# The first expert pair's gather written channel-major in two halves, with the router's sums ahead of the kept rows, the expert totals in a bank of their own and one early weight chunk moved up

## The reference

```python
h = h + cross_attn(rmsnorm(h, norm_xattn), ...)
h = h + moe(rmsnorm(h, norm_moe), lw)
# moe: logits = x @ w_router + b_router; top 4 of 32; softmax over the 4
# each expert e, on its own tokens:
gu = xb @ w_gate_up[e] + b_gate_up[e]        # 1024 -> 2048
gate, up = split(gu); glu = min(gate, 7) * sigmoid(1.702 * min(gate, 7))
y = ((clip(up, -7, 7) + 1) * glu) @ w_down[e] + b_down[e]   # 1024 -> 1024
out[token] += gate_weight * y
```

## Time and profile before

| | us |
|---|---|
| timed runs | 1409.6, 1412.96, 1413.68 |
| their median | 1412.96 |
| the profiled execution's span, first to last instruction | 1407.9 |
| from the first expert stage to the end, in that execution | 485.7 to 1407.9 |
| PE busy (matmul), share of the span | 98% |
| DMA, mean rate over the span | 353 GB/s |

### The profile page before, as it was taken

How to read it: one execution, slowest core, us unless ns; L and a number is a source line. 1 busy time by engine, 2 the same in 40 slices (tenths; PEclk the granted TensorE clock), 3 DMA queues, 4 the chain that set the end, 5 groups by cost and what they waited for, 6 DMA issues and landing times.

```text
span 1407.9 us, 16140 instructions
## 1 busy us (share of the span) xinstructions
PE 1376.7 (98%) x6438; PEld 673.5 (48%) x6438; DVE 441.5 (31%) x902; ACT 217.9 (15%) x403; POOL 27.9 (2%) x48
## 2 busy tenths in 40 slices
PE   9999999999999999999999999999999999999997
PEld 7788887677757633333333333333333332332322
DVE  5634345871461312221211312212113121121213
ACT  2220022052123411110101111011011010110102
POOL 0000002200000000000000000000000000000000
PEclk9999999999999999999999999999999999999999
DMA  7644446975379799999999999999999999999995
GB/s 256 210 154 154 175 142 200 376 268 190 118 283 398 284 413 428 429 425 430 427 430 427 430 427 429 428 429 429 428 428 429 430 427 430 427 430 426 431 426 228
DMA packets 71575, 497.25 MB, mean 353 GB/s; under 512 B 8752, under 2 KB 10216, under 8 KB 46824
## 3 DMA queue, kind: packets, MB, share of 16 engines
q1 hardware_dynamic: 65180, 477.94, 82.5%
q0 software_dynamic: 4432, 15.53, 3.0%
q10 hardware_dynamic: 1924, 3.23, 0.7%
HBM read 488.61 MB, written 8.24 MB: 353 GB/s over the span
## 4 chain that ended last, share of the span: by engine, by line
PE 83%; DMA 14%; DVE 2%; issue 1%; ACT 0%; SPq 0%; DVEq 0%
PE bank L1492 78%; DMA ring<-in_w_gate_up 8%; DMA flat<-in_w_gate_up 6%; PE bank L1503 4%; DVE wide L1418 1%; DMA flat<-in_x_prompt 0%; DVE wide L1475 0%; ACT wide L618 0%; PE bank L1946 0%; ACT L628 0%; ACT L658 0%; ACT wide L609 0%; SPq L506 0%; DVE wide L1466 0%; DVE wide L1395 0%
## 5 line engine op out<-in xcount | busy, mean ns | idle before, releaser
L1492 PE MATMUL bank<-ring,wide 128*64 128x512 f32 (+2 forms) x1696 | 405.5, 595 | 6.9 <-DMA ring<-in_w_gate_up 6.0
L1492 PE MATMUL bank<-wide 128*64 128x512 f32 (+6 forms) x1024 | 283.3, 574 | 8.7 <-DVE wide L1418 6.3
L1492 PE MATMUL bank<-tokT,ring 128*128 128x264 f32 x1152 | 266.0, 389 | 0.8 <-DVE tokT L959 0.8
L1492 PEld LDWEIGHTS bank<-ring,wide 128*64 128x64 f32 (+2 forms) x1696 | 132.4, 140 | 259.9 <-issue 246.1
L1492 PEld LDWEIGHTS bank<-tokT,ring 128*128 128x128 f32 x1152 | 217.8, 191 | 42.4 <-issue 6.4
L1492 PEld LDWEIGHTS bank<-wide 128*64 128x64 f32 (+4 forms) x1024 | 94.6, 152 | 171.9 <-issue 121.9
L609 ACT ACTIVATE wide<-bank 64x512 f32<-64x512 f32 (+3 forms) x104 | 58.2, 560 | 348.3 <-PE bank L1492 227.0
L1442 DVE TENSOR_SCALAR wide<-bank 128x512 f32<-128x512 f32 x32 | 22.1, 692 | 274.3 <-PE bank L1492 274.3
L1492 PE MATMUL bank<-flat,wide 128*64 128x512 f32 (+2 forms) x408 | 92.3, 589 | 3.7 <-DMA flat<-in_w_gate_up 3.7
L1492 PE MATMUL bank<-conv,wide 128*64 128x512 f32 (+1 forms) x400 | 91.1, 596 | 0.3 <-ACT wide L609 0.3
L890 ACT ACTIVATE wide<-wide 128x512 f32<-128x512 f32 x32 | 20.2, 630 | 428.6 <-DVE wide L1442 428.6
(11 more groups left out here) (257 smaller groups left out, 735.1 us busy)
## 6 DMA issues: line engine op xcount, KB each, us to landing
ring<-in_w_gate_up SPq DMA_DIRECT2D x64, 2048.0 KB, 26.1
ring<-in_w_down SPq DMA_DIRECT2D x32, 2048.0 KB, 28.1
flat<-in_w_gate_up SPq DMA_DIRECT2D x16, 2048.0 KB, 26.9
conv<-in_w_gate_up SPq DMA_DIRECT2D x16, 2048.0 KB, 25.5
wide<-in_w_gate_up SPq DMA_DIRECT2D x16, 2048.0 KB, 25.7
tokT<-in_w_gate_up SPq DMA_DIRECT2D x16, 2048.0 KB, 27.0
ring<-in_w_in SPq DMA_DIRECT2D x15, 2048.0 KB, 12.3
wide<-in_w_down SPq DMA_DIRECT2D x8, 2048.0 KB, 25.2
```

The lines of the kernel that those rows point to most:

```text
L1492: last[0] = pe.matmul(out, lhsT, rhs, start=start, stop=stop)
```

## The change

1. `PLAN` and PE's program: `sum_tokens` and the last `route` and `turn_tokens` now stand ahead of all the kept rows, `rs` ahead of `rt`, and `mrow` 0 stands with `mrow` 1 to 3. On ACT, `mrow` 0 is emptied after the scaled tokens instead of before the root.
2. The totals of the experts get a job of their own, `total` (bank 5), closed after `rank`. DVE makes the first `selT` before it reads the totals. The three filler matmuls between `rank` and the gather are gone; the other two write bank 4.
3. The first pair's gather is written with the operands exchanged (`gather_turned`): tokens as the stationary operand, selT as the moving one, so that the result is channel-major at once. Each half is twelve fp32 matmuls of 128 columns. The first half stands ahead of the first stage, the second half **between the first and the second stage**. ACT's two copies to `xgt` and the eight transposes are gone for this pair. DVE spreads the first half before its work on the number of passes, the second half after it.
4. The first pair's chunk of place 6 is issued after that of place 0 instead of after the last projection block; `first_acts` lies 520 columns further on, and `gT` and `onehot` before it.
5. Each engine reads the number of passes after the first pair (SP after the eighth refill).

```diff
-("xo", 3, D_, (1, 0)), ("mrow", 1, A_, (0,)),
-         ("rt", 3, D_, (2, 6, 7)), ("rs", 1, A_, (1,)), ("xtok", 3, A_, (3, 4, 5)), ("mrow", 3, A_, (1, 6, 7)),
-         ("srow", 2, A_, (0, 3)), ("rank", 1, D_, (2,))]
+("xo", 3, D_, (1, 0)),
+         ("rs", 1, A_, (1,)), ("rt", 3, D_, (2, 6, 7)), ("xtok", 3, A_, (3, 4, 5)), ("mrow", 4, A_, (0, 1, 6, 7)),
+         ("srow", 2, A_, (0, 3)), ("rank", 1, D_, (2,)), ("total", 1, D_, (5,))]
...
-            for j, name, k in ((2, "so", 1), (4, "so", 1), (5, "so", 3), (0, "so", 3), (1, "xo", 3), (3, "xo", 7)):
+            for j, name, k in ((2, "so", 1), (4, "so", 1), (5, "so", 3), (0, "so", 3), (6, "so", 3), (1, "xo", 3), (3, "xo", 7)):
                 filled(sp, name, k)
                 first_chunk(FIRST_SLOT.index(j))
-            first_chunk(3)
...
-            move("mrow", 0, mrows[0][:, 0:512], 512, 11)
             b = filled(s, "rs")
...
                 copy(xtok[0:n, t, :], acc[0:n, t, :], rr[0:n, t:t + 1]).then_inc(S["xtok_ready"], 1)
-            for k in range(1, 4):
+            for k in range(4):
                 move("mrow", k, mrows[k // 2][:, k % 2 * 512:k % 2 * 512 + 512], 512, 11)
...
+            def gather_turned(h):
+
+                for i in range(4):
+                    for t in (0, 1):
+                        rows = xtok[:, t, 512 * h:512 * h + 512].rearrange("p (s d m) -> p s m d", d=P, m=2)
+                        mm(bank[4 + h][:, i * P:i * P + P], rows[:, i // 2, i % 2, :], selT[:, t, :], t == 0, False)
+                    rows = slice(32 * h, 32 * h + TS)
+                    ends = xtok[rows, 2, 0:512].rearrange("p (s d m) -> p s m d", d=P, m=2)
+                    mm(bank[4 + h][:, i * P:i * P + P], ends[:, i // 2, i % 2, :], selT[rows, 2, :], False, True)
+                last[0].then_inc(S["xgt_turned"], 1)
...
-            gather(1)
+            pe.wait_ge(S["sel_ready"], 1)
+            gather_turned(0)
             emptied(pe, "srow", 1)
-            pe.wait_ge(S["bias_in"], 112)
             pe.wait_ge(S["crossed_in"], 96)
             hidden_bias(first_pair, 0)
-            turn_rows(1)
-            pe.wait_ge(S["bias_in"], 112)
-            pe.wait_ge(S["passes_ready"], 1)
-            n = pe.value_load(npass[0:1, 0:1], min_val=0, max_val=MAXP - 1)
+            emptied(pe, "total")
...
                 gate_up(0, 0)
+                if first:
+                    gather_turned(1)
                 gate_up(0, 1)
```

More of the change, by code:

```diff
@@ L908, in experts @@
                 if not final:
[L909 removed]
+                    copy_rows(at(2, 1))
                 copy_turned(1)
@@ L1370, in _, with mark, spread_half @@
                                          in1=msk[0:TS, 2], op0=ALU.add, op1=ALU.mult)
-            st(ins)
+            done(ins, "rank")
+            emptied(v, "rank")
             v.wait_ge(S["consts_set"], 2)
             select(0)
-            done(v.tensor_reduce(small[0:1, 0:1], b[0:1, 3 * E:4 * E], AX.X, ALU.max), "rank")
+            v.tensor_tensor(out=gts, in0=lg, in1=top[:, :, 0:1].to_broadcast([P, 3, E]), op=ALU.subtract)\
+                .then_inc(S["lg_ready"], 1)
+            b = filled(v, "total")
+            done(v.tensor_reduce(small[0:1, 0:1], b[0:1, 0:E], AX.X, ALU.max), "total")
+            def mark(pair, buf):
+                v.tensor_copy(onehot[:, buf].rearrange("p (j c) -> p j c", j=2), bc(id4[:, bass.ds(pair * 2, 2)], CAP))\
+                    .then_inc(S["onehot_ready"], 1)
+            mark(0, 0)
+            def spread_half(n, h):
+                v.wait_ge(S["xgt_turned"], n + (h + 1))
+                v.tensor_tensor(out=xg[:, 4 * h:4 * h + 4, :], in0=bank[4 + h][:, :].rearrange("p (k n) -> p k n", k=4),
+                                in1=bc(gmoe[:].rearrange("p s m -> p (s m)")[:, 4 * h:4 * h + 4], P), op=ALU.mult)\
+                    .then_inc(S["xg_ready"], 1)
+            v.wait_ge(S["bias_in"], 112)
+            spread_half(0, 0)
             for p in range(1, MAXP + 1):
                 st(v.tensor_scalar(rkp[:, :, p * E:p * E + E], rkp[:, :, 0:E], float(-CAP * p), None, ALU.add))
-            emptied(v, "rank")
+            emptied(v, "total")
             st(v.tensor_scalar(small[0:1, 1:2], small[0:1, 0:1], float(CAP), None, ALU.is_gt))
@@ L1428, in experts @@
                 if not final:
-                    v.wait_ge(S["xy_full"], at(2, 2))
+                    if not first:
+                        v.wait_ge(S["xy_full"], at(2, 0))
                     select(at(2, 2))
@@ L1945, in stay_warm @@
                 for _ in range(times):
-                    pe.matmul(bank[5][:, 0:256], ident[:], bgu[:, 0:256], start=True, stop=True)
+                    pe.matmul(bank[4][:, 0:256], ident[:], bgu[:, 0:256], start=True, stop=True)
             pe.wait_ge(S["bias_in"], 112)
@@ L1953, in _ @@
                     turn_tokens(j - 1)
+            sum_tokens()
+            route(KB - 1)
+            turn_tokens(KB - 1)
             pe.wait_ge(S["raw_kept"], 1)
             cache_rows("mrow", 0, kept_x, 11)
-            route(KB - 1)
-            sum_tokens()
-            turn_tokens(KB - 1)
             cache_rows("mrow", 1, kept_x, 11)
```

44 lines of the change are left out of this document (18 added, 26 removed).

## The result

The change made the kernel slower: 1422.26 us median (four runs, 1421.37 to 1423.70) against 1412.87 (four runs, 1409.60 to 1413.68). The two medians differ by 9.4 us, a quotient of 1.0066. The ratio given with these runs, which isn't the quotient of their medians, is 1.0079, 95% interval 1.0065 to 1.0094, and it agrees with later runs of the kernel before: their medians are 1410.7 to 1411.0, so that 1422.26 is 1.0080 to 1.0082 of them. The forecast was 1414.7, within 1409.5 to 1419.0: the time lies above the range. The profiled execution has a span of 1421.7 us, 13.8 more than the one of before; that is more than the medians show, because the profile of after is its slowest run (1423.70), and that of before lies near its fastest (in the runs of after and all later ones the time is 1.8 to 2.2 us above the span).

A forecast was written before the change was run, and what follows sets the result against it. DMA bounds the end through the eighth refill: +3.3 (bank 0) - 0.9 (totals), 3.5 won from gather to stage 1, 2.8 lost at the second half, so 1412.96 + 1.7 = 1414.7 us, range 1409.5 to 1419.0.

The forecast's parts named there:

- What sets the end: Whole kernel: DMA sets the end through the eighth refill, which waits for stage 9 of the first pair.
- Router's sums first: PE ahead of the kept rows: logits start 0.9 us earlier, mask ready at 473.8 instead of 474.8.
- Kept rows together: PE ahead of the ranks: waits for ACT to empty bank 0, idle 3.8 us; ranks start 3.3 us late.
- Totals apart: Between ranks and gather: DVE no longer waits for the totals, 0.9 us won back.
- Early chunk: DMA ahead of the first pair: the idle gap moves behind the ninth chunk; counts nothing.
- number of passes: Reading it after the first pair: costs nothing if under 3.8 us on the refills it delays.
- Gather with operands exchanged: First pair: 2.8 us a half; stage 1 1.1 us earlier than now, stages 2 to 9 1.7 us later.
- upper bound of 5.2 a half: Exchanged gather: no overlap of load and stream, 0.43 us a matmul, 5.2 us a half.
- rival at 7%: Exchanged gather: reading every second column leaves loads unhidden, 5.2 us a half, 1419.5 us; 7%.
- The clock: PE after the bank 0 gap: clock falls to half, +3 to +7.5 us, most likely +4.7, 1417.7 us; 15%.
- the forecast's base of 1412.96: Median time of the kernel before, to which the forecast added 1.7 us.

The follow-up runs named there:

- order_warm: order_only with nine filler matmuls in front of the job that waits for bank 0, so PE waits but isn't idle; 1414.59 us, ratio 1.0021 to before.
- free_fill: bank_free with three filler matmuls back between the totals and the second srow job; 1412.96 us, ratio 1.0007 to before.
- no_ends: free_fill without the four 8-row matmuls of each gather half, so eight sample tokens don't reach the first pair; 1408.35 us, ratio 0.9985 to before.
- ends_last: free_fill with each half's eight 128-row matmuls first, then its four 8-row ones, into a bank opened by one zero-weight matmul; 1412.82 us, ratio 1.0011.
- contiguous: bank_free with the first gather's tokens read as adjacent columns instead of every second one (computes something else); 1411.55 us, ratio 1.0010 to before.
- order_only: Kernel before with only the sums ahead of the kept rows, mrow 0 among these and emptied late by ACT; 1420.53 us, ratio 1.0060.
- order_again: The same kernel as order_only, run again for another profile; the profiled run took 1415.70 us.
- warm_gap: The changed kernel with nine filler matmuls ahead of the job that waits for bank 0; 1421.45 us, ratio 1.0075 to before.
- bank_free: The changed kernel with srow 0 in bank 3 and srow 1 in bank 0 behind ranks and totals; 1413.21 us, ratio 1.0012 to before.
- chunk_only: The kernel before with only the chunk of place 6 issued early and its place moved; 1411.43 us, ratio 0.9997 to before.

## Why the prediction was wrong

**What sets the end: right.** DMA, through the eighth refill; its 13.73 us and the span's 13.8 agree, and so do the other profiles.

**Router's sums first: right in sign, small.** They start at 469.02 instead of 469.38, although the last `turn_tokens` ahead of them came 0.46 us later in this profile. The ranks waited for the bank and not for the mask, so nothing of it counted.

**Kept rows together, +3.3: right in mechanism.** Idle time 3.91 us against 3.8 forecast, the place and the engine as forecast; ACT's first copy ran from 476.35. By `order_warm` the wait costs 3.9 us at the median. At full clock the ranks would start at 478.82, against the forecast 478.15.

**Totals apart, -0.9: right** (-0.94 at full clock). **Early chunk and number of passes, 0: right.** SP's reading stands between the eighth and the ninth refill, which are 3.76 us apart as before in every profile.

**Gather with operands exchanged: mis-sized.** The term took the scan's 0.23 us for each matmul, 2.8 a half; at full clock the halves took 4.34 and 4.45 (`free_fill`). What the nearest row lacked was the alternation of 128-row and 8-row weights, shown by `no_ends` and `ends_last`. The upper bound of 5.2 a half, given to loads that aren't hidden, held it; but it was used only for a rival at 7%, and the reason it gave (every second column) was wrong by `contiguous`. This adds 1.5 us ahead of the first stage and 1.6 behind it: at full clock the change would have cost 1.7 + 3.1 = 4.8, and the table's 5.5 with the 0.7 by which the ranks came later than forecast (0.46 of it from ahead of the seam). With these alone the time would have stayed inside the range, at some 1418.5.

**The clock: the step that failed.** The sum took the clock at 1.00 throughout, and the fall stood only as a rival. It was given 15%, because the gap seemed hardly longer than the time after which the clock had fallen at the kernel's end, and because PE is dense around it. It fell in this profile and in both profiles of the order alone, each time in the gap (at 476.3, 475.5 and 476.9). And its price was too low: up to 3.0 us for kept rows, fillers and ranks, taken as the likeliest, and at most 2.8 more for the first half. In `order_only` and `order_again` the clock was back 3 us after PE went on. In the kernel after it wasn't: 20 us at half, and by the table 8.2 us lost. Of these, kept rows, fillers and ranks are 2.3, the first half and the bias matmuls behind it 4.1 (7.56 - 4.34 = 3.2 in the half alone), and the first stage 1.75. The rival had the fall and its place right and its end wrong: it lacked the bias matmuls and the first stage. Why the clock stayed at half for so long is open.
The Trainium skill, "TensorE: Matmul & The Clock Gate", section "What's actually happening", says that an idle TensorE is throttled to half rate and a busy one released. The fall in the gap of 3.91 us agrees with the idle part. The 19.6 us of PE shown busy at 0.50 don't agree with the busy part, and neither do the falls in `warm_gap` and `bank_free`, where PE was never idle for more than 0.53 us.

**The loss by the medians.** It is 9.4 us by the runs of the result, about 11.5 by the later runs of before; the forecast's base of 1412.96, from three runs, lay 2 us above these. Of the loss, by the single edits, the wait is 3.9, the exchanged gather about 2.3 (`bank_free` 2.4, `free_fill` 2.3), and the rest, 3 to 5, is left for the clock. The 8.2 us of the table are those of the slowest run.

## What to carry to other kernels

Where a job list ties the order to the banks, moving a job also moves the moment at which its bank is free again: look for the next writer of that bank and what is queued behind it, and give the bank to a job that isn't on the path, which here won back 9 of 11 us. Where PE will wait for some 4 us, price the work behind the wait with the clock at half as a case of its own, and don't count on its quick return: here it was back after 3 us in two profiles and after 20 us in a third. And a price per matmul taken from another row is good only if the row has the same sequence of shapes: here an 8-row matmul between 128-row ones cost more by the changes around it than by its work (some 0.34 of 0.57 us).

## What the runs showed that was not expected

- The clock fell with PE never idle for more than 0.53 us: at 477.8 in `bank_free` and 483.7 in `warm_gap`, both in the exchanged gather, and at 469.9 to 470.5 in `warm_gap`, `order_warm`, `no_ends` and `ends_last`, in or just ahead of the transposes of the last token rows and the kept rows. In `chunk_only`, whose program on PE is that of the kernel before, it stood at 0.50 in 472 to 474, where the profile of before has 1.00. In the profile of after it also fell at 8.7 us, with PE busy. The falls in the gather lasted some 10 us and ended in the first stage, those near 470 and in `chunk_only` 3 to 4 us. `free_fill` and `contiguous`, with the same gather, stayed at 1.00. What decides between them is open; the seam of the kernel before does the one and the other with the same code.
- After the same idle time and ahead of the same kept rows, fillers and ranks, the clock was back after 3 us in `order_only` and after 20 in the kernel after. The exchanged gather never stood at the moment of a return in any profile; whether it keeps the clock low or only happened to meet it wasn't tried apart from the rest.
- A change between 128-row and 8-row weights costs some 0.19 us at full clock in this gather. The load itself takes the same for either, 196 and 190 ns in `free_fill`:

```profile
L1497 PEld LDWEIGHTS bank<-wide 128*128 128x128 f32 x16 | 2.2, 196 | 0.4
L1497 PEld LDWEIGHTS bank<-wide 8*128 8x128 f32 x8 | 1.2, 190 | 0.5
```
